# Two layers of a hybrid Mamba-2, Hyena and mLSTM backbone with 32 experts: a half-integer Hyena transform, packed expert tiles, and more slots for expert weights

## What is computed

```python
def bidir_long_conv(z, h_fwd, h_bwd):
    L, ch = h_fwd.shape                       # 256, 256
    two_sided = jnp.concatenate([h_fwd, jnp.zeros((1, ch)), h_bwd[1:][::-1]], axis=0)
    two_sided = two_sided / jnp.sum(jnp.abs(two_sided), axis=0, keepdims=True)
    zf = jnp.fft.rfft(z, n=2 * L, axis=1)
    hf = jnp.fft.rfft(two_sided, n=2 * L, axis=0)
    return jnp.fft.irfft(zf * hf[None], n=2 * L, axis=1)[:, :L]

def hyena_mixer(u, p):
    v, *gates = jnp.split(short_conv(u, p['hy_conv_w'], p['hy_conv_b']), 3, axis=-1)
    filt = hyena_filters(u.shape[1], p)
    z = v
    for order, gate in enumerate(gates):
        z = gate * (bidir_long_conv(z, filt[:, 0, order], filt[:, 1, order]) + p['hy_skip'][order] * z)
    return z

def hier_moe(h, p):                           # top-1 group of 4, then top-2 of its 8 experts
    ...
    for g in range(N_GROUPS):
        hid = silu(einsum('td,edf->tef', t, w_gate[g])) * einsum('td,edf->tef', t, w_up[g])
        out = out + einsum('tef,efd->td', hid * gate_w[..., None], w_down[g])
```

## Time and profile before

| | us |
|---|---|
| median of three runs | 1380.37 (1379.44 to 1391.26) |
| span of the profiled execution | 1376.8 |
| start, modulation and first filters | 0 to 60 |
| layer 0: in-projection with Hyena | 60 to 300 |
| layer 0: scans, out-projection, router | 300 to 496 |
| layer 0: expert loop | 496 to 780 |
| layer 1: start and in-projection | 785 to 940 |
| layer 1: scans, out-projection, router | 940 to 1103 |
| layer 1: expert loop | 1103 to 1357 |
| read back, last norm, output | 1357 to 1377 |

### The profile page before, as it was taken

How to read it: one execution, slowest core, us unless ns; L and a number is a source line. 1 busy time by engine, 2 the same in 40 slices (tenths; PEclk the granted TensorE clock), 3 DMA queues, 4 the chain that set the end, 5 groups by cost and what they waited for, 6 DMA issues and landing times. The chain is left out here.

```text
span 1376.8 us, 20166 instructions
## 1 busy us (share of the span) xinstructions
PE 1222.0 (89%) x7844; PEld 803.2 (58%) x7844; DVE 632.2 (46%) x1246; ACT 302.6 (22%) x616; POOL 128.0 (9%) x144
## 2 busy tenths in 40 slices
PE   6899999999989989998887689998889999988882
PEld 3544547987678865554454366567767755554451
DVE  4334773137863643532322364853285543433334
ACT  4102012254543202121111132122452200000001
POOL 0000000000000012221212100000000112222210
PEclk9999999999989989999999899999999999999897
DMA  8743133146641559999999755340574679999982
GB/s 294 207 143 122 61 107 92 51 134 215 205 154 37 221 172 396 390 384 375 379 383 371 290 168 166 123 138 20 176 255 151 248 308 397 397 399 392 401 329 109
DMA packets 150167, 322.21 MB, mean 234 GB/s; under 512 B 28667, under 2 KB 111672, under 8 KB 127672
## 3 DMA queue, kind: packets, MB, share of 16 engines
q1 hardware_dynamic: 138584, 304.86, 61.0%
q0 software_dynamic: 11392, 15.77, 3.6%
q10 hardware_dynamic: 96, 0.26, 0.0%
HBM read 321.11 MB, written 21.23 MB: 249 GB/s over the span
## 5 line engine op out<-in xcount | busy, mean ns | idle before, releaser
L659 PE MATMUL bank<-hT,ring 128*128 128x512 f32 (+1 forms) x544 | 206.8, 538 | 1.9 <-DVE hT L1768 1.8
L659 PE MATMUL bank<-ring,hT 128*128 128x256 f32 (+1 forms) x928 | 182.0, 351 | 4.2 <-ACT hT L1400 2.1
L659 PE MATMUL bank<-ring,qkT 128*64 128x256 f32 x816 | 163.1, 407 | 22.3 <-DMA ring<-in_moe_w_up 10.4
L659 PEld LDWEIGHTS bank<-ring,hT 128*128 128x128 f32 x928 | 155.4, 195 | 23.6 <-ACT hT L1400 2.5
L659 PEld LDWEIGHTS bank<-hT,ring 128*128 128x128 f32 x544 | 104.2, 193 | 98.5 <-issue 90.9
L1772 DVE TENSOR_TENSOR xbc<-xbc,bank 64x256 f32<-64x256 f32 x65 | 27.5, 423 | 254.8 <-ACT xbc L1400 204.7
L659 PEld LDWEIGHTS bank<-ring,qkT 128*64 128x64 f32 x816 | 96.6, 147 | 48.7 <-issue 17.3
L659 PE MATMUL bank<-hT,qkT 128*64 128x256 f32 x416 | 99.8, 416 | 10.4 <-DMA zotok<-in_moe_w_up 5.9
L1400 ACT ACTIVATE xbc<-bank 64x256 f32<-64x256 f32 x65 | 24.6, 378 | 358.9 <-PE bank L659 287.6
L1332 POOL DMA_INDIRECT pair_rows<-hyT,zotok x65 | 60.0, 923 | 409.6 <-DVE xbc L1778 378.5
L659 PEld LDWEIGHTS bank<-hT,qkT 128*64 128x64 f32 x416 | 56.2, 150 | 24.7 <-issue 13.8
(11 more groups left out here) (337 smaller groups left out, 1816.7 us busy)
## 6 DMA issues: line engine op xcount, KB each, us to landing
ring<-in_w_mod SPq DMA_DIRECT2D x40, 1024.0 KB
ring<-in_moe_w_down SPq DMA_DIRECT2D x27, 1024.0 KB
ring<-in_moe_w_gate SPq DMA_DIRECT2D x26, 1024.0 KB
ring<-in_moe_w_up SPq DMA_DIRECT2D x25, 1024.0 KB
ring<-in_w_in SPq DMA_DIRECT2D x22, 1024.0 KB
hT<-in_moe_w_up SPq DMA_DIRECT2D x14, 1024.0 KB
hT<-in_moe_w_down SPq DMA_DIRECT2D x13, 1024.0 KB
hT<-in_moe_w_gate SPq DMA_DIRECT2D x12, 1024.0 KB
```

The lines of the kernel that those rows point to most:

```text
L659: return nc.tensor.matmul(o, a, b, start=s, stop=e, **k)
```

## The change

**Hyena.** The transform is taken at half-integer frequencies, with even and odd tokens apart. A spectrum of 256 frequencies is then even part plus odd part for the lower 128 and their difference for the upper 128. So `hyena_spectra` has four products of one matmul each, and `filter_step(l, 5)` four of one in place of five of two. ACT copies the two odd products to SBUF (`odd_spectra`, placed before the third silu of its loop), DVE forms sums and differences before and after the multiplication: 20 operations per order for 12. `hyena_back` has matmuls of 128 columns for those of 256. Token order is strided by two in the transposes and in `gated_filter`. The tables shrink from five of 256 KB to two, `dft` and `inv`.

**Slots.** The freed columns are `spare`. There are 19 slots for 14; slots 14 to 18 are used in the loop as long as it runs, and layer 0 begins with 15 matrices, layer 1 with 18.

**Expert loop.** Gathered rows take turns between the lower and upper 64 partitions, which frees `big[:, 2048:4096]` for slot 14. The product silu(gate) x up is formed in place. The down result keeps its place in 128 partitions: one operation weights it, ACT's in layer 0 (`weighted`) and DVE's in layer 1, and the scatter sends 128 half rows of 2 KB (`pair_of` is doubled and 1 added for the upper half). In layer 1 the gate row is formed in the same layout.

The core of the diff; left out are the DVE side of the filter spectra (per pair a copy, a sum and a difference), the constants and the loops for further items, which follow the same layout:

```diff
-ONCE = ((8, 9, 10), (11, 12, 8, 9, 13, 10))
-FIRST_ORDER = ((8, 9, 6, 7, 0, 1, 2, 3, 10, 4, 5), (11, 12, 8, 9, 6, 13, 7, 0, 1, 2, 3, 10, 4, 5))
+ONCE = ((8, 9, 18, 10, 15, 16, 14), (11, 12, 8, 9, 13, 10, 15, 16, 17, 14))
+FIRST_ORDER = ((8, 9, 18, 6, 7, 0, 1, 2, 3, 10, 15, 16, 4, 5, 14), (11, 12, 8, 9, 6, 13, 7, 0, 1, 2, 3, 10, 15, 16, 17, 4, 5, 14))
+PLACES = 19
...
-    return s < MOE_SLOTS or (n <= LAST_IN_TAPS if l == 0 else s in (8, 9, 10, 11))
+    return s < MOE_SLOTS or s >= 14 or (n <= LAST_IN_TAPS if l == 0 else s in (8, 9, 10, 11))
...
-        rows_v = xn_v
+        rows_v = big[:, 0:2048].rearrange("p (u d) -> p u d", u=2)
         rowsT_v = qkT[:, 0:2 * KB * ITEM_ROWS].rearrange("p (u k n) -> p u k n", u=2, k=KB)
-        sg_v = xbc[:, 0:2 * EH].rearrange("p (u n) -> p u n", u=2)
-        hid_v = xbc[:, 512:512 + 2 * EH].rearrange("p (u n) -> p u n", u=2)
-        hidT_v = xbc[:, 1024:1024 + 4 * ITEM_ROWS].rearrange("p (u f n) -> p u f n", u=2, f=2)
-        res_v = hyT[:, 0:2 * D].rearrange("p (u n) -> p u n", u=2)
+        hid_v = xbc[:, 0:2 * EH].rearrange("p (u n) -> p u n", u=2)
+        hidT_v = xbc[:, 512:512 + 4 * ITEM_ROWS].rearrange("p (u f n) -> p u f n", u=2, f=2)
+        res_v = hyT[:, 0:D].rearrange("p (u n) -> p u n", u=2)
+        pair_halves = pair_rows.rearrange("n (h d) -> (n h) d", h=2)
+        gate_halves = grow[:, D:D + 512]
...
-            (x[:, 0:2048],), (dftc[:, :], dfts[:, :], dftn[:, :], invc[:, :]),
-            (hfilt[:, 1024:2048], invs[:, :], keep[:, :])]
+            (x[:, 0:2048],), (spare[:, 0:1024], dft[:, :], inv[:, :]),
+            (hfilt[:, 1024:2048], spare[:, 1024:1536], keep[:, :]),
+            (big[:, 2048:4096],), (hyT[:, 1024:2048], vaug[:, 1024:1536], hsum[:, 1024:1536]),
+            (state[:, 0:512], zotok[:, 512:1024], xbc[:, 1024:1536], hfilt[:, 2048:2560]),
+            (big[:, 4096:4608], wgr[:, :], hfilt[:, 512:1024], grow[:, 0:512]), (spare[:, :], big[:, 4096:4608])]

...
-                    if s in (8, 9, 13):
+                    if s in (8, 9, 13, 18):
...
-                    elif s == 10:
+                    elif s in (10, 15, 16, 17):
                         sp.wait_ge(*due(("x attended", l, MIX_ORDER[l][-1])))
+                    elif s == 14:
+                        for u in range(2):
...
-                    if old[0] == "down":
-                        pe.wait_ge(*due(("read left", old)))
...
-                    for m, (src, mat) in enumerate((("s", dftc_v[:, :, 0:P]), ("s", dftc_v[:, :, P:L]),
-                                                    ("d", dfts_v[:, :, 0:P]), ("d", dfts_v[:, :, P:L]),
-                                                    ("s", dftn_v[:, 0, :, :]))):
-                        if m not in parts:
-                            continue
+                    for m in parts:
+                        q, r = m // 2, m % 2
                         b = product(("spec", l, m))
                         pe.wait_ge(*due(("tapsd", l)))
-                        for t in range(2):
-                            rhs = taps_v[:, t, 0, :, :] if src == "s" else tabs_v[t][:, 0, :, :]
-                            last = mm(b[:, :], mat[:, t, :], rhs, t == 0, t == 1)
-                        last.then_inc(pe_done, made(("spec", l, m)))
+                        rhs = tabs_v[r][:, 0, :, :] if q else taps_v[:, r, 0, :, :]
+                        mm(b[:, :], dft_v[:, q, r, :], rhs).then_inc(pe_done, made(("spec", l, m)))

             for l in range(DEPTH):
                 t0 = 0 if l == 0 else 2
...
-                                                           hy_v[:, c, s * L + t * P:s * L + (t + 1) * P], ident[:, :])
+                                                           hy_v[:, c, s * L + t:(s + 1) * L:2], ident[:, :])
                         last.then_inc(pe_done, made(("hz", l, o, s)))

                 def hyena_spectra(o):

-                    for n, mat in enumerate((dftc_v[:, :, 0:P], dftn_v[:, 1, :, :], dftc_v[:, :, P:L],
-                                             dfts_v[:, :, P:L])):
-                        b = product(("zf", l, o, n))
-                        pe.wait_ge(*due(("zt", l, o)))
-                        for t in range(2):
-                            last = mm(b[:, n0:512], mat[:, t, :], zt_v[:, t, n0:512], t == 0, t == 1)
-                        last.then_inc(pe_done, made(("zf", l, o, n)))
+                    for q in range(2):
+                        for r in (1, 0):
+                            b = product(("zf", l, o, q, r))
+                            pe.wait_ge(*due(("zt", l, o)))
+                            mm(b[:, n0:512], dft_v[:, q, r, :], zt_v[:, r, n0:512]).then_inc(pe_done, made(("zf", l, o, q, r)))

                 def hyena_back(o):

...
-                            for q in range(4):
-                                inv = invc_v if q < 2 else invs_v
-                                last = mm(b[:, s * L:(s + 1) * L], yf_v[:, q, s * L + c * P:s * L + (c + 1) * P],
-                                          inv[:, q % 2, :], q == 0, q == 3)
+                            for r in range(2):
+                                for q in range(2):
+                                    last = mm(b[:, s * L + r * P:s * L + (r + 1) * P],
+                                              zs_v[:, 2 * q + r, s * L + c * P:s * L + (c + 1) * P], inv_v[:, q, r, :],
...
+                    if (l, n) == (1, 1):
+                        b = product(("grow", l, n, 1, 0))
+                        pe.wait_ge(*due(("gate bias", l, n)))
+                        for q in range(2):
+                            last = mm(b[64 * q:64 * q + 64, :], gate_four[:, 0:1].broadcast_to([P, 64]),
+                                      modrow(5)[:, 512 * q:512 * q + 512])
+                        last.then_inc(pe_done, made(("grow", l, n, 1, 0)))
+                        return
...
+                    r0 = j % 4 // 2 * R
                     for k in range(KB):
-                        last = nc.tensor.transpose(b[:, k * R:(k + 1) * R], rows_v[0:R, j % 4, k * P:(k + 1) * P],
-                                                   ident[0:R, 0:R])
+                        last = nc.tensor.transpose(b[:, k * R:(k + 1) * R], rows_v[r0:r0 + R, j % 2, k * P:(k + 1) * P],
+                                                   ident[r0:r0 + R, r0:r0 + R])
...
-                return nc.gpsimd.indirect_dma_start(pair_rows, bass.IndirectOffsetOnAxis(at_, 0), src, None,
-                                                    bounds_check=MOST_PAIRS - 1, oob_is_err=False)
+                return nc.gpsimd.indirect_dma_start(pair_halves, bass.IndirectOffsetOnAxis(at_, 0), src, None,
+                                                    bounds_check=2 * MOST_PAIRS - 1, oob_is_err=False)
...
+                def odd_spectra(o):
+                    for q in range(2):
+                        act.wait_ge(*due(("made", ("zf", l, o, q, 1))))
+                        fn(zs_v[:, 2 * q + 1, n0:512], bank(("zf", l, o, q, 1))[:, n0:512], ACT.Copy,
+                           ("read", ("zf", l, o, q, 1)), ("odd", l, o, q))
...
+                    if blk == 2:
+                        odd_spectra(0)
...
-                def left_half(j):
...
+                def weighted(j):
...
-                    fn(res_v[0:R, j % 2, 0:512], bank(("down", l, j))[0:R, :], ACT.Copy, ("read left", ("down", l, j)),
-                       ("result", l, j, "act"), scale=weight_of[0:R, j:j + 1])
+                    fn(res_v[:, j % 2, :], bank(("down", l, j))[:, :], ACT.Copy, ("read", ("down", l, j)),
+                       ("result", l, j), scale=weight_of[:, j:j + 1])
...
-                        act.wait_ge(*due(("hid", l, j - 2)))
+                        act.wait_ge(*due(("made", ("hidden", l, j - 2))))
                     act.wait_ge(*due(("made", ("gate up", l, j))))
-                    fn(sg_v[0:R, j % 2, :], bank(("gate up", l, j))[0:R, 0:EH], ACT.Silu, ("sg", l, j))
+                    fn(hid_v[0:R, j % 2, :], bank(("gate up", l, j))[0:R, 0:EH], ACT.Silu, ("sg", l, j))
...
+                    zr, zr_h, zi, zi_h = (spec(zs_v[:, k, n0:512]) for k in range(4))
+                    yr, yr_h, yi, yi_h = (spec(yh_v[:, k, n0:512]) for k in range(4))
+                    a = spec(ht1[:, n0:512])
+                    for q, (low, high) in enumerate(((zr, zr_h), (zi, zi_h))):
+                        dve.wait_ge(*due(("made", ("zf", l, o, q, 0))))
+                        dve.wait_ge(*due(("odd", l, o, q)))
+                        even = spec(bank(("zf", l, o, q, 0))[:, n0:512])
+                        tt(low, even, high, ADD)
+                        tt(high, *((high, even) if q else (even, high)), SUB, ("read", ("zf", l, o, q, 0)))
+                    for k, (r_, i_, yr_, yi_) in enumerate(((zr, zi, yr, yi), (zr_h, zi_h, yr_h, yi_h))):
+                        tt(yr_, r_, filt(k), MUL)
+                        tt(a, i_, filt(2 + k), MUL)
```

(19 more changed lines are left out.)

## The result

The changed kernel takes 1372.4 us (median of 12 runs, 1369.0 to 1378.2), the kernel before beside it 1380.6 (1377.3 to 1391.3): a ratio of 0.9922, with a 95% interval of 0.9899 to 0.9945. That is 8 us less (a second comparison gave 0.9932), where 22.4 had been forecast. The profiled span is 1370.7 us for 1376.8.

A forecast was written before the change was run, and what follows sets the result against it. TensorE was taken to bound the in-projection with Hyena, weight loads the expert loops. Terms -1.4 - 4.6 - 1.7 - 14.0 - 0.75 = -22.4 from 1380.4 gave 1358.0 us; own range 1348 to 1367, with rivals 1340 to 1374.

The forecast's parts named there:

- term 4: Expert loops: four more matrices in store at the start of each shorten each loop by 7.0 us, -14.0 in all.
- the contention at the door of layer 1's loop: Before the expert loop: the first gather lands beside weights instead of on idle engines, +1 us per loop.
- Terms 1 to 3: Start and Hyena stages of both layers: -1.4, -4.6 and -1.7 us, 7.7 us together.
- Term 1: Start: 0.5 MB fewer table loads bring TensorE's awaited parameter sooner, -1.4 us, bounds 0 and -3.3.
- Terms 2 and 3: Hyena in layers 0 and 1: shorter TensorE spectra and way back, less waits and slow clock, -4.6 and -1.7 us.
- The price of small pieces: Expert loops: slots 15 to 18 load in pieces of 2 to 6 KB per partition, costing 2.5 us in each loop.
- Term 5: End of layer 1: packed results need one operation over 128 partitions, halving 1.53 us, -0.75; elsewhere hidden under weight waits.
- B: Expert loops: the store does not pay, extra matrices only shift the queue, giving 1373 us; chance 0.13.
- C: Expert loops: gathered and scattered rows spread over more DMA engines, intervals shorten, giving 1340 us; chance 0.14.
- D: Expert loops: half rows fall on fewer DMA engines, 8 KB more per item on late ones, giving 1379; chance 0.08.
- E: Expert loops: half rows put 16 KB more per item on the late DMA engines, +42, giving 1399 us; chance 0.04.
- F: Hyena stages of both layers: the chain eats its gain, giving 1364 us; chance 0.06.

The follow-up runs named there:

- e2: Changed kernel with the old first matrices and slots (11 and 14 matrices in store, slots 14 to 18 not used): 1379.6 us, 0.9949 to the kernel before.
- e1: Kernel before with only the Hyena part of the change, slots and expert loop as before: 1382.1 us, 0.9987.
- e8: Hyena-only kernel with VectorE's two xbc convolutions placed before the scan exponents: 1368.0 us, 0.9917 to the kernel before.
- e7: Changed kernel with late loads of slots 14 and 17, convolutions before the scan exponents, and early odd copies: 1346.9 us, 0.9762 to the kernel before.
- e10: Changed kernel with seven extra matmuls of unused result before the modulation vector in each layer: 1367.1 us, 0.9896 to the kernel before.
- e12: Changed kernel with convolutions first and early odd copies, but the old slots and store: 1359.9 us, 0.9836 to the kernel before.
- e3: Changed kernel with matrices of slots 14 and 17 loaded only after the first gathered rows landed: 1362.2 us, 0.9833 to the kernel before.
- e11: Changed kernel with late loads, convolutions first and early odd copies, slots 15 to 18 filled only once: 1350.1 us, 0.9794 to the kernel before.
- e4: Changed kernel with VectorE's two xbc convolutions moved ahead of the scan exponents: 1360.0 us, 0.9798 to the kernel before.
- e13: Changed kernel with twelve extra matmuls in TensorE's wait near 60 us, before layer 0's in-projection: 1369.4 us, 0.9890 to the kernel before.
- e14: Changed kernel with late loads, convolutions first, early odd copies and twelve extra matmuls at the start: 1351.2 us, 0.9770 to the kernel before.

## Why the prediction was wrong

The direction was right and the time lies within the range, but only near its upper end; the sum is 14 us too large. Most of it is term 4: its four matrices brought 2 to 4 us for 14 (e2). By the table the loops gained 10.9 us for 16, and the stages in front of them lost 7.6 for 2; the failed step that is known is the contention at the door of layer 1's loop, which cost about 5 us and not 1. Terms 1 to 3 brought some 2 us for 7.7 (e1), since the slow clock behind waits was charged once per layer and came behind each. The range of 1348 to 1367 "from the bounds of terms 2 to 4" doesn't follow from the text, as term 4 has no bounds; the time lies above it.

**Term 1, -1.4, measured -0.4.** The sign that it named, the end of TensorE's wait by 58.5, did not come: the wait ended at 60.4 and 59.7 us in the two profiles of the changed kernel, at 59.9 and 60.9 before. The step that failed is that 0.5 MB less in the queue brings the parameter sooner. SP issues it at 57.0 and 56.4 us, for 56.6 and 57.6 before, behind a row of small loads that it issues one every 0.34 us, while the DMA engines are 19% busy from 50 to 55 us in both kernels. So what comes before it there is SP's issuing, not bytes. Before, and in the changed kernel:

```profile
56.62 0.43 SPq L406 DMA_DIRECT2D rb<-in_exp_router_b  x1
```

```profile
57.00 0.43 SPq L407 DMA_DIRECT2D rb<-in_exp_router_b  x1
```

I also wrote that TensorE's saved 5 us lie behind a wait of 3.28 us and so cost nothing. They made the wait 5.90 us, and the matmuls behind it slower (20 records in 11.52 us; 24 took 12.23), by about 1 us, which falls into the next stretch. A wait that I counted as cover had a price of its own.

**Terms 2 and 3, -6.3, measured -3.0 in their stages (-4.6 in e1).** The waits were right: 1.75 us (forecast 1.7) before the way back, 3.58 (4.0) and 3.06 us before the modulation vector; filtered(0) waits for ScalarE's copies. Their times were not: the row is there at 216.5 us, not 214.4, and TensorE comes to it at 213.1, not 210.4. The step that failed is the clock: I charged 1.7 us once per layer. In layer 0's stage the mean clock fell from 0.99 to 0.96, 0.03 x 2 x 185 = 11 us more at the lower level, 5.5 of matmul time. It is low behind each of the three waits: 0.80 from 60 to 75 us, 0.83 from 150 to 160, 0.66 from 216 to 226. The slow stretches behind the first two came before filtered(1), which starts at 191.95 and so 1.2 us sooner than the 193.15 of the kernel before, where I had 3.3; its operations, and VectorE's and ScalarE's work behind them, took as long as forecast. A second step is not settled: I took the rest of the layer as shifted by what the stage gains, and in e1 layer 1's scans took 3.5 us longer than the mean of before, but with the same Hyena part they took 168.6 in e2 and 164.4 in e8. TensorE's mean clock over the span was 0.924 in e1, 0.928 in the changed kernel, 0.941 to 0.945 in the kernel before, 0.942 in e7. e10 supports the clock as the cause: matmuls that do nothing useful, put into two of the waits, make the kernel faster by 5 us.

**Term 4, -14.0, measured -2 to -4 in the changed kernel (e2) and -10 with late loads (e12).** Layer 0 was right: -6.7 and +1.3 for -8 and +1. In layer 1 the table has 4.2 us for 8 in the loop. Over all profiles the loops were nearer to the forecast: on average 273.1 and 243.2 us in the six with the old slots and 266.0 and 236.3 in the ten with the new ones, 7.1 and 6.9 us less. The term that failed is the contention at layer 1's door, +1: from the issue of the first gather to the first gate and up product take 9.7 and 10.1 us in the two profiles of the changed kernel, 5.1 in both of the kernel before, and 6.1 with late loads. TensorE waits 3.03 us for the rows, which land behind the weights that fill the idle stretch, and the loop begins at the low clock. I read that stretch as free for four matrices, 10.5 us of traffic, and did not ask what is issued inside it; the gather is, at 1097.89 in the kernel before. e3 moves two matrices behind it and wins it back. The price of small pieces, 2.5 us per loop, was of the right size in the intervals of e7 and e11 (9.30 to 9.16 us and 8.78 to 8.62, over 13 starved items: 2 us) and did not show in the time.

**Term 5, -0.75, measured -1.4 at the end.** The last operations of VectorE take 0.75 us each where two took 1.53. The packing is worth 0.9949 against 0.9987, 5 us by these ratios and 2.5 by the medians, with intervals that overlap. Whether it is more than its visible 1.4 us is not settled.

**The rivals.** B named 1373, and the time came out there. In the changed kernel the store paid little, as B says, but not for its reason: the loops got 6.7 and 4.2 us shorter, the stages in front of them took 1.3 and 6.3 back, and with late loads the store pays 10 us (e12). C, D and E fall by e2: equal traffic, intervals and loops. What I worked out for D from the Trainium skill ("DMA: Bandwidth & Descriptors", section The descriptor swizzle) therefore changed nothing here, and no run shows the engines one by one. F was near the truth for terms 2 and 3, but VectorE's chain took only part of the gain; the clock took the rest.

Of the other page cited: the Trainium skill ("TensorE: Matmul & The Clock Gate", section LDWEIGHTS) gives 107 ns for a weight load of 128 columns. In e7, at full clock, the way back starts at 147.80 and the next product at 151.47: 3.67 us for 32 records, 115 ns each. That is nearer to the page than to the 0.14 us that I took from the transposes, so the way back was worth 0.8 us more per order than forecast.

**What is open.** e3 gained more than its stretches show. Part of it stands in unchanged code around 60 us, where the first matmuls of the in-projection find the clock high or low. The wait before them does not decide it alone: behind 2.92 us (e3) they ran at full clock, behind 3.12 (e1), 5.55 (e4) and 5.90 us they did not. e13 and e14 did not settle how much of that reaches the end. Nor is it known why e4 gained 17 to 19 us by the ratios where its stretches show 12.

## What to carry to other kernels

Where an engine that is the bound loses work, draw its timeline anew and look for the places where it now arrives early: each is a wait, and each of the five waits listed in the section on the result was followed by microseconds at the lower clock, which cost 2.6 us behind the wait of 3.06. Mend these places, by order on the feeding engines, before judging the change: the same Hyena part was worth 2 us or 11 by where two convolutions stood. An idle stretch of the DMA engines is free only for transfers that end before the next urgent one is issued inside it.

## What was not expected of the hardware

More work made the kernel faster: 14 extra matmuls (3.0 us per layer) in TensorE's waits, 0.9896 for 0.9932 (e10). A gather of 64 rows took 7.7 us from issue to use, 3.2 on idle engines. It was issued 6.4 us after the last of the eleven matrices that SP issued from 1066.92 us on, and by the GB/s of the windows 2.8 MB were moved in those 7.7 us, the gathered rows among them. And a second profile of the same program differed by 3.8 us in one stretch (165.6 and 169.4 us), where its granted clock was 0.94 and 0.92: a stage difference of that size between two single profiles needs a second pair. The part of it ahead of the first gather took, in all sixteen profiles and in no order by kernel, 159.3 to 160.5, 162.3 to 162.5 or 164.3 to 165.4 us and nothing between; why it comes in three groups is not known.
